# Down projection of the first feed-forward: the hi and lo product rows side by side in one matmul

## The reference

```python
h = rms_norm(x, norm2_w)
u = causal_dwconv(h @ w_up, ffn_conv_w, ffn_conv_b)
u_gate, u_val = jnp.split(u, 2, axis=-1)
return x + (jax.nn.silu(u_gate) * u_val) @ w_down      # w_down: 5632 x 2048
```

## Time and profile before

| what | value |
|---|---|
| median of 3 runs | 2460.87 us (2457.59 to 2462.07) |
| the profiled execution's own time | 2461.01 us |
| its span in the trace | 2459.3 us |
| TensorE matmul busy | 2438.0 us (99%), 25716 matmuls |
| VectorE busy | 1662.5 us (68%), 2174 instructions |
| ScalarE busy | 1204.6 us (49%) |
| DMA engines, mean busy share | 55% |
| mean granted TensorE clock | 0.999 |

### The profile page before, as it was taken

How to read it: one execution, slowest core, us unless ns; L and a number is a source line. 1 busy time by engine, 2 the same in 40 slices (tenths; PEclk the granted TensorE clock), 3 DMA queues, 4 the chain that set the end, 5 groups by cost and what they waited for, 6 DMA issues and landing times.

```text
span 2459.3 us, 61026 instructions
## 1 busy us (share of the span) xinstructions
PE 2438.0 (99%) x25716; PEld 2350.1 (96%) x25716; DVE 1662.5 (68%) x2174; ACT 1204.6 (49%) x1450; POOL 59.5 (2%) x69
## 2 busy tenths in 40 slices
PE   9999999999999999999999999999999999999999
PEld 9989999999999999999999999999999999999997
DVE  7777666677777776688866555566766666666666
ACT  6656645555555555455623323446544444444444
POOL 0000000000000000004100000001000000000000
PEclk9999999999999999999999999999999999999999
DMA  7555456666666666665543333354655556555553
GB/s 232 171 150 155 150 168 187 198 196 189 194 190 195 188 188 203 191 192 171 162 122 105 98 106 97 105 163 150 211 188 188 187 188 193 189 189 188 188 179 137
DMA packets 397851, 420.57 MB, mean 171 GB/s; under 512 B 15422, under 2 KB 372530, under 8 KB 397554
## 3 DMA queue, kind: packets, MB, share of 16 engines
q1 hardware_dynamic: 397170, 416.46, 55.0%
q10 hardware_dynamic: 528, 1.84, 0.3%
HBM read 416.15 MB, written 2.10 MB: 170 GB/s over the span
## 4 chain that ended last, share of the span: by engine, by line
PE 94%; DVE 3%; ACT 1%; issue 1%; DMA 0%; SPq 0%; ACTq 0%
PE psum L2578 25%; PE psum L2580 25%; PE psum L2579 25%; PE psum L2594 3%; PE psum L2593 3%; PE psum L2592 3%; PE psum L3056 2%; PE psum L3162 1%; DVE w_lo L1384 1%; PE psum L3152 1%; PE psum L3281 0%; PE psum L3203 0%; PE psum L3287 0%; ACT w_hi L756 0%; PE psum L3003 0%
## 5 line engine op out<-in xcount | busy, mean ns | idle before, releaser
L2578 PE MATMUL psum<-act_hi,w_hi 128*128 128x256 f32 (+2 forms) x4736 | 1340.2, 283 | 3.5 <-DVE act_lo L1422 2.6
L2580 PE MATMUL psum<-act_hi,w_lo 128*128 128x256 f32 (+2 forms) x4736 | 1322.7, 279 | 0.8 <-issue 0.8
L2579 PE MATMUL psum<-act_lo,w_hi 128*128 128x256 f32 (+2 forms) x4736 | 1323.0, 279 | 0.0
L1384 DVE TENSOR_TENSOR w_lo<-raw,w_hi 128x1024 fp32r<-128x1024 f32 x788 | 960.6, 1230 | 454.5 <-ACT w_hi L756 454.4
L756 ACT ACTIVATE w_hi<-raw 128x1024 fp32r<-128x1024 f32 x788 | 828.2, 1058 | 882.0 <-PE psum L2580 739.4
L2578 PEld LDWEIGHTS psum<-act_hi,w_hi 128*128 128x128 f32 x4736 | 890.5, 188 | 12.3 <-issue 4.0
L2579 PEld LDWEIGHTS psum<-act_lo,w_hi 128*128 128x128 f32 x4736 | 891.4, 188 | 3.6 <-issue 2.2
L2580 PEld LDWEIGHTS psum<-act_hi,w_lo 128*128 128x128 f32 x4736 | 890.3, 188 | 0.0
L2578 PE MATMUL psum<-ff_hi_rows,w_hi 128*128 128x256 f32 x640 | 176.6, 276 | 0.0
L2579 PE MATMUL psum<-ff_lo_rows,w_hi 128*128 128x256 f32 x640 | 176.6, 276 | 0.0
L2580 PE MATMUL psum<-ff_hi_rows,w_lo 128*128 128x256 f32 x640 | 176.6, 276 | 0.0
(11 more groups left out here) (429 smaller groups left out, 1921.3 us busy)
## 6 DMA issues: line engine op xcount, KB each, us to landing
raw<-in_w_in SPq DMA_DIRECT2D x188, 512.0 KB, 3.8
raw<-in_w_up SPq DMA_DIRECT2D x176, 512.0 KB, 4.5
raw<-in_w_down SPq DMA_DIRECT2D x176, 512.0 KB, 4.1
raw<-in_w_gate_up SPq DMA_DIRECT2D x176, 512.0 KB, 3.5
raw<-in_w_out SPq DMA_DIRECT2D x64, 512.0 KB, 3.5
x_rows<-in_x SPq DMA_DIRECT2D x8, 256.0 KB, 6.9
out_x<-out_rows SPq DMA_DIRECT2D x8, 256.0 KB, 2.6
raw<-in_w_in SPq DMA_DIRECT2D x4, 384.0 KB, 3.7
```

The costliest lines, as they stand in the source:

```text
L1384: dve.tensor_tensor(w_lo[:, slot], raw[:, slot], w_hi[:, slot].bitcast(F32), ALU.subtract).then_inc(S["lo_done"], 1)
L2578: pe.matmul(out_, wh, xh, start=first and r == 0, stop=False)
L2579: pe.matmul(out_, wh, xl, start=False, stop=False)
L2580: mm = pe.matmul(out_, wl, xh, start=False, stop=last and r == RK - 1)
```

## The change

The hi and lo rows of a chunk lie in one tile (`ff_rows`, `last_rows`, [2, 4*256+64]), with the padding that they had. A new `halves_unit` takes the place of `unit` in the downs of the first feed-forward: w_hi goes into the array once for each (r, c), and one matmul moves the 256 hi columns and the 256 lo columns past it into the 512 columns of a bank; a second matmul moves the hi columns past w_lo and adds into the bank's first half. A unit has 16 matmuls. VectorE's `leave_down` becomes two instructions of 128x512 (2 banks x 256): the first adds the first halves of the two banks to the residual, the second, after a wait for the first on a new semaphore `half_added`, adds the second halves and signals `evicted`.

```diff
--- before.py
+++ after.py
@@ -261,8 +261,7 @@
         [
             ("up", [8, T3], F32), ("conv", [8, T1], F32), ("ff", [4, T1], F32),
             ("squares2", [8, T2], F32), ("row_pad", [48], F32),
-            ("ff_hi_rows", [4 * T1 + 64], F32R), ("ff_lo_rows", [4 * T1 + 64], F32R),
-            ("last_hi_rows", [4 * T1 + 64], F32R), ("last_lo_rows", [4 * T1 + 64], F32R),
+            ("ff_rows", [2, 4 * T1 + 64], F32R), ("last_rows", [2, 4 * T1 + 64], F32R),
             ("out_rows", [2, D], F32),
             ("row_ss", [2, 8], F32),
         ],
@@ -308,10 +307,11 @@
 
     def rows_of_four(name):
 
-        return M[name][:, 0:4 * T1].rearrange("p (k t) -> p k t", t=T1)
-
-    FF_HI, FF_LO = rows_of_four("ff_hi_rows"), rows_of_four("ff_lo_rows")
-    LAST_HI, LAST_LO = rows_of_four("last_hi_rows"), rows_of_four("last_lo_rows")
+        return M[name][:, :, 0:4 * T1].rearrange("p h (k t) -> p h k t", t=T1)
+
+    FF, LAST = rows_of_four("ff_rows"), rows_of_four("last_rows")
+    FF_HI, FF_LO = FF[:, 0], FF[:, 1]
+    LAST_HI, LAST_LO = LAST[:, 0], LAST[:, 1]
 
     proj = M["proj"]
     psum = nc.alloc_psum_tensor("psum", [P, 8, 512], F32)
@@ -1856,18 +1856,23 @@
                         return
                     leave(v + 4 * j + 4, (pair0 + j) % 2, up[:, 2 * j:2 * j + 2, 0:T], T)
 
-                def leave_down(v, d):
-                    leave(v + d + 1, (pair0 + d) % 2, resid[:, 2 * d:2 * d + 2, TC1], T1,
-                          how="added")
+                def leave_down(v, d, i):
+                    pair, t = (pair0 + d) % 2, resid[:, 2 * d:2 * d + 2, TC1]
+                    dve.wait_ge(S["unit_used"], v + d + 1)
+                    dve.tensor_tensor(t, psum[:, 2 * pair:2 * pair + 2, 0:T1], t, ALU.add) \
+                        .then_inc(S["half_added"], 1)
+                    dve.wait_ge(S["half_added"], 8 * i + (d + 1))
+                    dve.tensor_tensor(t, psum[:, 2 * pair:2 * pair + 2, T1:2 * T1], t, ALU.add) \
+                        .then_inc(S["evicted"], 1)
 
                 def leave_rows(v, g):
                     leave(v + 2 * g + 2, (pair0 + g) % 2, f_rows[:, :, 512 * g:512 * g + 512], 512,
                           how="added")
 
-                def downs_leave(v, d):
+                def downs_leave(v, d, i):
 
                     if not by_rows:
-                        leave_down(v, d)
+                        leave_down(v, d, i)
                         lo(v + 4 + d, d % 4)
                     else:
                         lo(v + 4 + d, d % 4)
@@ -1924,13 +1929,13 @@
                     v = u + 24 * i - 8
                     while_up(i, v)
                     for d in range(8):
-                        downs_leave(v + 16, d)
+                        downs_leave(v + 16, d, i - 1)
                 i = FCH - 1
                 w = u + 24 * i + 8
                 while_up(i, w - 16, last=True)
 
                 for d in range(8):
-                    downs_leave(w, d)
+                    downs_leave(w, d, i - 1)
                     if vals and d < 4:
                         taps(i, 4 + d, 1)
                     elif d == 4:
@@ -1942,7 +1947,7 @@
             def norm_on(w, pair0, leave_down):
 
                 for d in range(8):
-                    leave_down(w + 8, d)
+                    leave_down(w + 8, d, FCH - 1)
                     lo(w + 12 + d, d % 4)
                     norm_pair("n2", c_premix, TC2, d - 1)
 
@@ -2580,6 +2585,18 @@
                     mm = pe.matmul(out_, wl, xh, start=False, stop=last and r == RK - 1)
                 return mm
 
+            def halves_unit(u, slot, pair, x):
+
+                pe.wait_ge(S["lo_done"], u + 1)
+                for r in range(RK):
+                    for c in range(2):
+                        out_ = psum[:, 2 * pair + c].rearrange("p (h t) -> p h t", h=2)
+                        at = 256 * r + P * c
+                        wh, wl = w_hi[:, slot, at:at + P], w_lo[:, slot, at:at + P]
+                        pe.matmul(out_, wh, x[:, :, r], start=r == 0, stop=False)
+                        mm = pe.matmul(out_[:, 0], wl, x[:, 0, r], start=False, stop=r == RK - 1)
+                mm.then_inc(S["unit_used"], 1)
+
             def rows_unit(u, slot, pair, hi_, lo_, k0, first, last):
 
                 pe.wait_ge(S["lo_done"], u + 1)
@@ -2909,7 +2926,7 @@
                         else:
                             group(v + 4 * j, g + j, (pair0 + j) % 2, xs, T)
 
-                def downs(v, g, i, hi_, lo_):
+                def downs(v, g, i, x):
                     pe.wait_ge(S["ff_fflo"], i + (n0 + 1))
                     if by_rows:
                         for d in range(8):
@@ -2918,12 +2935,12 @@
                                 bank_free(g + n)
                             elif k == 0:
                                 pe.wait_ge(S["last_left"], 2 * n - 2)
-                            rows_unit(v + d, d % 4, (pair0 + n) % 2, hi_, lo_, 2 * k, k == 0,
+                            rows_unit(v + d, d % 4, (pair0 + n) % 2, x[:, 0], x[:, 1], 2 * k, k == 0,
                                       k == 1)
                         return
                     for d in range(8):
                         bank_free(g + d)
-                        unit(v + d, d % 4, (pair0 + d) % 2, hi_, lo_, 0, T1, True, True)
+                        halves_unit(v + d, d % 4, (pair0 + d) % 2, x)
 
                 if by_rows:
                     for r in range(RK):
@@ -2957,7 +2974,7 @@
                         group(u + 4 * j, g0 + j, (pair0 + j) % 2, xs, T)
                 with pe.Fori(1, FCH) as i:
                     ups(u + 24 * i - 8, gp * i - (gp - 4) + g0)
-                    downs(u + 24 * i + 8, gp * i - (gp - 8) + g0, i - 1, FF_HI, FF_LO)
+                    downs(u + 24 * i + 8, gp * i - (gp - 8) + g0, i - 1, FF)
                 if by_rows:
                     for n in range(8):
                         c, tt = divmod(n, 2)
@@ -2969,7 +2986,7 @@
                                            ident[:], start=k == 0, stop=True, is_transpose=True,
                                            skip_group_check=True)
                         mm.then_inc(S["h_rows"], 1)
-                downs(u + 24 * FCH - 8, g0 + gp * FCH - (gp - 4), FCH - 1, LAST_HI, LAST_LO)
+                downs(u + 24 * FCH - 8, g0 + gp * FCH - (gp - 4), FCH - 1, LAST)
                 if by_rows:
                     pe.wait_ge(S["h_copied"], 5)
                     for _ in range(WARM):
```

## The result

The changed kernel takes 2490.15 us (median of 4, 2486.97 to 2492.28), the kernel before 2459.97 in the same comparison: ratio 1.0123, 95% interval 1.0110 to 1.0136. It is slower, as forecast, but by 30 us where 7.8 were forecast, and it lies outside the range.

A forecast was written before the change was run, and what follows sets the result against it. It took TensorE, busy for 99% of the span, as the bound, with VectorE deciding at the end of the stage. The profiled 2461.0 us + 6.5 (VectorE) + 1.3 (TensorE) gave 2468.8 us; range 2460 to 2474.

The forecast's parts named there:

- TensorE's term: First feed-forward's downs, nine chunks at TensorE's pace: each pair of 256-column matmuls made one of 512 costs 2.3 ns more, +1.3 us.
- upper bound: Upper limit on the cost of widening matmuls in the first feed-forward's downs: three times the 2.3 ns, +4 us, an estimate.
- The end of the stage: D0 to I3, behind the first feed-forward's loop: VectorE has only 5.0 us free, so I3 starts 6.5 us later.
- the walk: VectorE's queue followed instruction by instruction from D0 to I3: L0 3.6 us later, I3 6.5 us later in all.
- The second add: VectorE's eviction of each down unit: one more add, +0.725 us a unit, 88 times; nothing comes of it in the loop.
- rival 3: VectorE falls behind in the loop's downs too: 6 us more, 2475 us; chance 0.03.
- Rival 1: In the downs, 512-column matmuls stream faster than the trace's rows show: up to -7.7 us, 2459.8 us; chance 0.20.
- Rival 2: TensorE's clock falls after L7's wait at the end of the stage: 1.7 us lost, 2470.5 us; chance 0.10.
- Rival 4: The end of the stage costs less, +4.6 us, as VectorE's wait is free and TensorE's path decides: 2465.6 us; chance 0.09.
- Rival 5: In the downs the 512-column matmul streams like two of 256: +6.5 us alone, 2467.5 us; chance within the forecast's 0.58.

The follow-up runs named there:

- the grouped one: The changed kernel with each unit's eight wide (512-column) matmuls first, then its eight narrow (256-column) ones: 2470.47 us, ratio 1.0037 to the kernel before.

## Why the prediction was wrong, step by step

- **TensorE's term (+1.3 us) is the step that failed**, by 21.7 us. "A pair becomes 2.3 ns dearer" took the row of 512 columns behind 512 columns and the row of 256 behind 256 as prices of two forms that can be added. The pair is 13.3 ns dearer, 353.3 against 340; that is 9 x 64 x 13.3 ns = 7.7 us. It is even outside the upper bound, +4 us, which was three times a difference that had nothing to do with it. The rest, 9 x 1.70 = 15.3 us, falls on instructions which the change doesn't touch, and no term of the sum stood for them. The clue was in the trace of before: L0 to L7 at 117.7 ns a matmul, in the last of the two chunks that the prediction left out of TensorE's pace.
- **The end of the stage (+6.5 us) was right**: 6.35 in the changed kernel; 6.4 us as a ratio with TensorE's part undone. Its two parts came at 3.6 and 2.75 for 3.6 and 2.9. Waits for a bank stood at D5 to D7 and at L7, where TensorE sat idle for 1.5 us. At D5 to D7 they set a unit back by 0.5 to 0.8 us, for 0.6 to 0.9 forecast. Of the one forecast at L6 at most 0.2 us showed; TensorE, at 2.83 us a unit instead of 2.74, came to it later. I3 waited 0.4 us for the last tile, where 0.7 was forecast. One printed step of the walk does not add up: 1110.0 and two units of 3.3 are 1116.6, not 1117.4. L1 has a norm pair (0.83) too, and with it the walk's own 1117.4 and all that follows are right.
- **The second add** cost 0.72 us start to start, for 0.725; in the loop it cost nothing (no wait of TensorE on it there), so rival 3 falls. The Trainium skill has a sentence that a semaphore between two Vector operations costs nothing extra (VectorE: DVE Perf Modes, The DRAIN you can't avoid). The traces here disagree by 0.12 us, 0.72 against 0.60.
- **Rival 1, the fast wide matmul**, falls: a wide matmul takes 235 ns in the changed kernel, and in the grouped one 226 at the head of a unit and 233 on average. The rule of the Trainium skill (TensorE: Matmul & The Clock Gate, Back-to-back issue gap) gives 215.8; no wide matmul of a down unit comes near it here.
- **Rival 2, the clock**: it stayed at 1.00 through the end of the stage, whose longest wait was those 1.5 us. Rival 4 falls with the 6.35.
- **Rival 5** had this much right: the wide matmul does not save anything. That two narrow ones are cheaper even so, 2466 against 2470 in its best order, was not foreseen.

Still open: why one real pair in the loop locks the slow pace while one behind the pause at L0, a pair into an idle bank, and wide-wide-narrow-narrow in the same banks fall back. The wide matmul that locks takes 226 ns; those that don't are followed by another wide one, or take 232 ns or more. Whether that is cause or sign no run here tells. So it is shown that the pairs bring the loss and that it lies in the pace of the stream; what inside TensorE sets the pace is not shown.

## What to carry to other kernels

A price per instruction from a steady stream holds for that stream: before summing prices for a mixed one, look in the trace for the same instruction at another pace (here 113.3 and 117.7 ns, under one granted clock), and add a case in which all of the stage moves to it. After a change to TensorE's order, compare the starts in stages that were **not** edited. And where an in-order engine such as VectorE here has 5 us free in a stretch, 11.6 us of added work cost the difference, however low its mean share.

## What was not expected of the hardware

At a granted clock of 1.00 a back-to-back stream of 128x128 by 256-column fp32r matmuls keeps one of two paces for hundreds of matmuls: 113.3 or 117.7 ns. The wide-narrow order moved it from the first to the second ten times out of ten in the run with the plain matmul, and a single pair did so in the one chunk where it met the fast stream in the loop, but not behind a pause. A plain float32 matmul moved it back nine times out of nine at one place and not at another. Behind a pause the same untouched instructions ran at either pace in two traces. The order wide-wide-narrow-narrow avoids the slow pace, and takes 2469.87 us where wide-narrow takes 2490.15.
